# Attention of the first block inside the weight streams of its two projections

## The reference

```
x = x + 0.5*swiglu(rms_norm(x), ffn1)                   # g1, d1
proj = rms_norm(x) @ w_in          # 2048 -> 4608       # i1
qa (8 heads), ka (2), va (2), qd (4x2), kd (4x2) of 128; vd (4) of 256
qa, ka, qd, kd: rms_norm over 128 with a gain, then rotary (all 128, or the first 32)
out_a = softmax(qa ka^T / sqrt(128)) va                 # 8 heads
out_b = (softmax(qd0 kd0^T / sqrt(128)) - lam * softmax(qd1 kd1^T / sqrt(128))) vd
out_b = rms_norm(out_b) * subln * 0.8                   # 4 heads of 256
x = x + concat(out_a, out_b) @ w_out                    # o1
x = x + 0.5*swiglu(rms_norm(x), ffn2)                   # g2, d2
```

## Time and profile before

| | |
|---|---|
| median of 3 runs | 3600.59 us (3595.43 to 3614.2) |
| the profiled execution's own time | 3595.78 us |
| its span | 3594.0 us |
| PE, DVE, ACT, POOL busy | 94%, 64%, 42%, 1% of the span |
| mean granted TensorE clock | 0.972 of 2.4 GHz |
| time before the span and after it | 1.78 us |

### The profile page before, as it was taken

One profiled execution on the slowest core, in us unless ns is written; L12 is line 12 of the kernel. 1 busy time (PEld: TensorE's weight loads), 2 busy tenths in 40 slices (PEclk: granted clock), 3 DMA queues, 4 the chain that ended last, 5 costly groups with the idle time before them and its releaser, 6 DMA issues.

```text
span 3594.0 us, 40384 instructions
## 1 busy us (share of the span) xinstructions
PE 3384.7 (94%) x15130; PEld 2720.3 (76%) x15130; DVE 2306.3 (64%) x4078; ACT 1526.1 (42%) x2780; POOL 37.2 (1%) x37
## 2 busy tenths in 40 slices
PE   8999999999748999999999999999899988999898
PEld 6888878878637788887887788888567776888566
DVE  6788887765665688887777435555354346645565
ACT  5444444544334544444555322222254334422354
POOL 0000000000000000000000000000100000000100
PEclk9999999999978999999999999999899999999899
DMA  7777777766404677777786323333202235533314
GB/s 270 254 260 259 257 258 254 256 210 194 146 0 129 228 253 259 262 260 258 261 266 204 123 87 94 94 100 100 74 1 94 83 129 146 167 101 108 109 60 163
DMA packets 286920, 613.76 MB, mean 171 GB/s; under 512 B 19394, under 2 KB 23682, under 8 KB 284804
## 3 DMA queue, kind: packets, MB, share of 16 engines
q1 hardware_dynamic: 280804, 596.26, 51.2%
q0 software_dynamic: 1584, 8.39, 0.7%
q10 hardware_dynamic: 4336, 6.52, 0.5%
HBM read 604.80 MB, written 6.29 MB: 170 GB/s over the span
## 4 chain that ended last, share of the span: by engine, by line
PE 78%; DVE 10%; DMA 6%; ACT 3%; issue 2%; ACTq 0%; SPq 0%; DVEq 0%
PE acc L353 23%; PE acc L355 23%; PE acc L354 23%; DMA raw<-ffn_w_gu 5%; DVE lo L348 3%; PE acc L2017 2%; PE acc L2043 2%; ACT hi L344 1%; DVE cgw L1084 1%; PE tp L2030 1%; DVE mw L1086 1%; PE tp L1985 1%; PE tp L1681 0%; DMA raw<-ffn_w_down 0%; DVE tm L1576 0%
## 5 line engine op out<-in xcount | busy, mean ns | idle before, releaser
L348 DVE TENSOR_TENSOR lo<-raw,hi 128x512 fp32r<-128x512 f32 x1808 | 1208.5, 688 | 967.1 <-ACT hi L344 960.4
L344 ACT ACTIVATE hi<-raw 128x512 fp32r<-128x512 f32 x1808 | 1117.0, 630 | 1613.2 <-PE acc L355 1310.4
L353 PE MATMUL acc<-hi,hT_hi 128*128 128x512 f32 x1760 | 704.7, 400 | 30.4 <-DVE hT_lo L1071 14.6
L353 PE MATMUL acc<-hi,h_hi 128*128 128x512 f32 x1696 | 668.7, 394 | 23.3 <-DVE lo L348 18.2
L354 PE MATMUL acc<-hi,hT_lo 128*128 128x512 f32 x1760 | 689.4, 392 | 0.0
L355 PE MATMUL acc<-lo,hT_hi 128*128 128x512 f32 x1760 | 689.0, 391 | 0.0
L354 PE MATMUL acc<-hi,h_lo 128*128 128x512 f32 x1696 | 662.7, 391 | 0.0
L355 PE MATMUL acc<-lo,h_hi 128*128 128x512 f32 x1696 | 662.6, 391 | 0.0
L353 PEld LDWEIGHTS acc<-hi,hT_hi 128*128 128x128 f32 x1760 | 332.7, 189 | 121.9 <-DVE hT_lo L1071 22.1
L353 PEld LDWEIGHTS acc<-hi,h_hi 128*128 128x128 f32 x1696 | 319.7, 189 | 102.7 <-DVE lo L348 31.5
L355 PEld LDWEIGHTS acc<-lo,hT_hi 128*128 128x128 f32 x1760 | 332.8, 189 | 70.7
(11 more groups left out here) (244 smaller groups left out, 2282.8 us busy)
## 6 DMA issues: line engine op xcount, KB each, us to landing
raw<-ffn_w_gu SPq DMA_DIRECT2D x352, 512.0 KB, 5.5
raw<-w_in SPq DMA_DIRECT2D x280, 512.0 KB, 3.8
mw<-wmt SPq DMA_DIRECT2D x192, 512.0 KB, 5.2
raw<-ffn_w_down SPq DMA_DIRECT2D x176, 512.0 KB, 5.3
raw<-w_out SPq DMA_DIRECT2D x96, 512.0 KB, 4.2
ball<-rpbx SPq DMA_DIRECT2D x8, 768.0 KB, 8.6
x_rest<-x POOLq DMA_DIRECT2D x2, 2048.0 KB, 9.6
x<-x_rest SPq DMA_DIRECT2D x2, 2048.0 KB, 8.7
```

What stands on the lines that cost most here:

```text
L344: act.activation(hi[:, g % RING, :], raw_piece(g), ACT.Copy).then_inc(S["hi_made"], 1)
L348: dve.tensor_tensor(lo[:, g % RING, :], raw_piece(g), hi[:, g % RING, :].bitcast(F32), ALU.subtract).then_inc(S["lo_made"], 1)
L353: pe.matmul(bank, act_hi, hi[:, slot, :], start=start, stop=False)
```

## The change

The attention has no stage of its own. Its steps are called from `at1_side(s)` on PE, ACT and DVE, s counting 16 per chunk of i1 and going on into o1 (s = 144 + i in o1's piece i). Tables say at which piece each step stands. The chunks of i1 come in another order, o1 walks its pieces in another order, the norm's factor of a query is no longer multiplied into the query but given to the exponential as a scale per row, squares of heads go to ACT, gains are folded into the rotary tables once, scores and probabilities use the banks `cg` and `tp` in place of `acc`, the DMAs of `at1_consts` are issued by POOL.

```diff
+ORDER = (2, 0, 1, 5, 3, 6, 4, 7, 8)          # chunks of i1
+S_AT = (50, 56, 62, 68, 76, 84, 90, 96, 105, 109, 117, 121, 130, 133, 136, 139)   # scores(q)
+D_AT = (116, 128, 140, 146)                 # difference(h)
+V_AT = (131, 136, 146, 151)                 # diff_values(h)
+T_AT = (42, 43, 46, 63, 69, 80, 83, 97, 103, 112, 115, 124, 127)                  # heads_turn(g)
+O_PARTS = ((1, 0, 8), (0, 0, 8), (1, 8, 4), (0, 8, 4), (0, 12, 4), (1, 12, 4), (2, 0, 16), (3, 0, 16))
 # ACT
-                if j == 12:
-                    at1_consts()
 def exps(q): ...
-  ACT.Exp, bias=nm[:, q % 2, t:t + 1], scale=SCALE, ...
+  ACT.Exp, bias=nm[:, q % 2, t:t + 1], scale=qsd[:, t, col:col + 1], ...
+def head_square(pos, t, h): ...    # one 128x128 Square with its row sum, 52 in all
+def at1_side(s):                   # ACT
+    pos, r = s // 16 - 1, s % 16
+    if 0 <= pos <= 6 and (5 <= r <= 8 if pos else 5 <= r <= 6):  ... two head_square
+    if s == 23: ... activation(lam, Exp)
+    for e in now((44, 76, 108, 124), s): ... activation(qsd, Sqrt)
+    for g in now(T_AT, s - 5): ... activation(qkT, Copy)
+    for q in now(S_AT, s - 6): exps(q)
+    for q in now(S_AT[0:8], s - 11): pt_copy(q)
+    for q in now(S_AT[0:8], s - 15): head_hi(q)
+    for h in now(D_AT, s - 6): pt_copy(8 + h)
+    for k in now((147, 159), s): ... activation(obs, Sqrt)
+    for h in now((155, 156, 166, 167), s): ... activation(oT_hi, Copy)
 # DVE
+def axial_tables(k): ...  def partial_tables(k): ...     # s = 20 to 23
+def swapped(pos, t): ...           # 2 products, 256 elements a row each (64 for qd, kd)
+def rotated(pos, t): ...           # product of 512, sum of 512 (128 for qd, kd)
+def k_scaled(pos, t): ...          # keys alone are multiplied by their factor
+def at1_side(s):                   # DVE
+    if s == 19: dve.wait_ge(S["rope_in"], 16 * 13) ... lambda sums
+    if pos == 0 and r in (8, 9): ... swapped(0, r - 8); rotated(0, r - 8)
+    if 1 <= pos <= 6 and 7 <= r <= 10: ... swapped or rotated, in turn
+    for q in now(S_AT, s - 5): maxes(q)
+    for q in now(S_AT[0:8], s - 7): normalise(q)
+    for q in now(S_AT[0:8], s - 16): head_out(q)
+    for h in now(D_AT, s): difference(h, 0)
+    for h in now(D_AT, s - 1): difference(h, 1)
+    for h in now(V_AT, s - 5): diff_out(h)
+    for h in now(V_AT, s - 6): diff_squares(h)
+    ...
 # PE
+def at1_side(s):
+    for g in now(T_AT, s): heads_turn(g)
+    for q in now(S_AT, s): scores(q)
+    for q in now(S_AT[0:8], s - 6): turn_p(q, pr1[0][:, q % 2])
+    for q in now(S_AT[0:8], s - 10): head_values(q)
+    for h in now(D_AT, s - 1): turn_p(8 + h, pr1[h % 2][:, 0])
+    for h in now(V_AT, s): diff_values(h)
+    for h in now((150, 151, 161, 162), s): diff_turn(h)
-pe.wait_ge(S["roped"], 1)          # and all of at1 between the streams
+for c, kt0, n in O_PARTS:          # o1
+    if kt0 == 0 and c == 1:
+        pe.wait_ge(S["oh_lo"], A_HEADS)
+    elif kt0 in (8, 12):
+        pe.wait_ge(S["tg_lo"], g0 + (2 if kt0 == 8 else 4))
+    ...
+    for cx in now((33, 40, 52), i): x_turn(phases["n3"], cx, ...)
 # POOL, behind gain_load(0) and ahead of ctx_load(0)
+pool.wait_ge(S["mod_done"], MODS)
+pool.dma_start(ropa[:, 0], ...)    # the 13 DMAs of at1_consts
```

More of the change, by code:

```diff
@@ L223, in build @@
         lam = keep("lam", [P, 8])
+        sm1 = keep("sm1", [P, 4, 2])
         mx = keep("mx", [P, 2, 2])
@@ L501, in _ @@
             load_down(down[0], phases["d1"], 6 * FC)
-            load_wide(win1, phases["i1"], 0, 9)
-            load_wide(wout1, phases["o1"], 0, 4)
+            for k, c in enumerate(ORDER):
+                load_wide(win1, phases["i1"], c, 1, False, k)
+            o_unit = phases["o1"].pieces // 2
+            for c, kt0, n in O_PARTS:
+                for u in range(n // 2):
+                    unit(o_unit, wout1[c, kt0 // 2 + u])
+                    o_unit += 1
             load_gu(gu[1], phases["g2"], MODS)
@@ L692, in _, with exps @@
             stream(phases["d1"].pieces, 4, DK, after=d1_side)
+            g0 = phases["at1"].groups
+            def exps(q):
+                act.wait_ge(S["m_ready"], q + 1)
+                if 2 <= q < 10:
+                    act.wait_ge(S["cg_done"], q - 1)
+                elif q >= 12:
+                    act.wait_ge(S["cg_done"], 9 + (q - 12) // 2)
+                rows, sums = p_rows(q)
+                for t in range(2):
+                    col = q_col(q)
+                    ins = act.activation(rows[:, t], cg[q % 2][:, t * L:(t + 1) * L], ACT.Exp,
+                                         bias=nm[:, q % 2, t:t + 1], scale=qsd[:, t, col:col + 1],
+                                         accum_out=sums[:, t:t + 1])
+                ins.then_inc(S["p_made"], 1)
@@ L767, in _ @@
-            stream(phases["o1"].pieces, 4, after=o1_side)
+            stream(phases["i1"].pieces, 9, after=lambda c, j: (i1_side(c, j), at1_side(16 * c + j)))
+            for i in range(LOOK, 64 + LOOK):
+                hi_piece(act, phases["o1"].pieces + i)
+                at1_side(9 * 16 + i)
+                if i == 35:
+                    act.wait_ge(S["hq_made"], 52)
+                for c in now((35, 40, 53), i):
+                    act.wait_ge(S["acc_taken"], phases["o1"].taken + 2 * (c + 1))
+                    x_squares(c)
+                for c in now((38, 45, 57), i):
+                    x_hi(phases["n3"], 2, c)
@@ L1180, in i1_side @@
                     dve.wait_ge(S["rs_made"], norms[0])
[L1182 to L1192, removed]
-                    link(ins)
@@ L1194, in _ @@
[L1194 to L1204, removed]
@@ new lines, in both_tiles, with axial_tables @@
+            def both_tiles(v, n):
+                return v.unsqueeze(1).broadcast_to([P, 2, n])
+            def axial_tables(k):
+                g = gbc[:, k].rearrange("p (b s n) -> p b s n", b=2, s=2)
+                dve.tensor_tensor(tA[:, k, 0], ropa[:, 0], both_tiles(gbc[:, k], HD), ALU.mult)
+                for t in range(2):
+                    dst, sn = (v.rearrange("p (b s n) -> p b s n", b=2, s=2) for v in (tA[:, k, 1, t], ropa[:, 1, t]))
+                    for hf in range(2):
+                        ins = dve.tensor_tensor(dst[:, :, hf, :], sn[:, :, hf, :], g[:, :, 1 - hf, :], ALU.mult)
+                link(ins)
@@ new lines, in partial_tables @@
+            def partial_tables(k):
+                g = gbc[:, 2 + k]
+                dve.tensor_tensor(tBc[:, k, :, 0:32], ropb[:, 0], both_tiles(g[:, 0:32], 32), ALU.mult)
+                dve.tensor_copy(tBc[:, k, :, 32:HD], both_tiles(g[:, 32:HD], HD - 32))
+                for hf in range(2):
+                    d0, d1 = 16 * hf, 16 * (1 - hf)
+                    ins = dve.tensor_tensor(tBs[:, k, :, d0:d0 + 16], ropb[:, 1, :, d0:d0 + 16],
+                                            both_tiles(g[:, d1:d1 + 16], 16), ALU.mult)
+                link(ins)
@@ new lines, in rotated @@
+            def rotated(pos, t):
+                nh, k, x = 4 if pos else 2, int(pos in (0, 3, 5)), qk_src(pos, t)
+                xv = x.rearrange("p (h n) -> p h n", n=HD)
+                cs = tA[:, k, 0, t] if pos < 3 else tBc[:, k, t]
+                link(dve.tensor_tensor(xv, xv, cs.unsqueeze(1).broadcast_to([P, nh, HD]), ALU.mult))
+                w = HD if pos < 3 else 32
+                ins = dve.tensor_tensor(xv[:, :, 0:w], xv[:, :, 0:w], rp2[:, 0:nh * w].rearrange("p (h n) -> p h n", n=w),
+                                        ALU.add)
+                if t == 1 and pos not in (0, 3, 5):
+                    ins.then_inc(S["roped"], 1)
+                else:
+                    link(ins)
@@ L1311, in x_add @@
+            stream(phases["i1"], 9, 2, proj_take, after=lambda c, j: (i1_side(c, j), at1_side(16 * c + j)))
             def x_add(c, t):
@@ L1313, in x_add @@
                 dve.tensor_tensor(xv, acc[2 * (c % 2) + t][:], xv, ALU.add).then_inc(S["acc_taken"], 1)
-            def o1_side(c, j):
-                if c and j == 8:
-                    x_lo(phases["n3"], 2, c - 1)
-            stream(phases["o1"], 4, 2, x_add, after=o1_side)
+            for i in range(LOOK, 64 + LOOK):
+                lo_piece(dve, phases["o1"].pieces + i)
+                at1_side(9 * 16 + i)
+                for c in now((39, 46, 58), i):
+                    x_lo(phases["n3"], 2, c)
+                for c in now((29, 33, 49, 65), i):
+                    for t in range(2):
+                        o_done_at(dve, phases["o1"], c, t)
+                        x_add(c, t)
             def second_lap(j):
@@ L1819, in turn_p @@
                 ins.then_inc(S["cg_done"], 1)
-            g0 = phases["at1"].groups
             def head_values(q):
-                pe.wait_ge(S["cg_taken"], 14 + q)
-                if q >= 2:
-                    pe.wait_ge(S["oh_lo"], q - 1)
-                c0 = VA_COL + q // 4 * HD
+                pe.wait_ge(S["cg_taken"], q + 1)
+                wait(pe, "oh_lo", q)
```

(43 more changed lines are left out.)

422 lines of the change are left out of this document (268 added, 154 removed).

## The result

The median fell from 3600.49 us (3595.43 to 3614.2, 4 runs) to 3500.07 us (3494.59 to 3507.94, 4 runs): ratio 0.9717, 95% interval 0.9684 to 0.975. The profiled execution is the longest of the four, 3507.94 us with a span of 3506.0.

A forecast was written before the change was run, and what follows sets the result against it. PE bounds the streams, a chain of round trips the attention. −136.0 − 3.0 − 5.3 + 43 + 4 = −97.3 us, from the profiled 3595.78 to 3498.5, so a median of 3500; range 3488 to 3524.

The forecast's parts named there:

- The hole: PE's gap between i1's last matmul and o1's first, over the attention: removed in full, −136.0 us.
- the slow start of o1: o1's first 20 pieces, whose first matmuls run at the lower clock level: removed, −3.0 us.
- ACT's issues: 13 DMA issues on ACT in i1's chunk 0, stopping PE, then half rate: moved to POOL, −5.3 us.
- PE's side work: Attention transposes, scores and values on PE within the streams, not hidden: +43 us, between 39.7 and 45.4.
- Stops: PE stops in the new stream where DVE or ACT bursts run late: +4 us, bounds 0 and 28.
- The stop of `turn_p(0)`: PE after piece 56, where turning the first probabilities waits for the normalisation: about 1.2 us.
- The stop after pieces 20 to 25: DVE's tables and chunk 0's rotary run some 3.2 us late, so PE stops for about 0.6 us.
- DVE by totals: Busiest chunk of i1, pieces 66 to 81: DVE 22.8 us beside PE's 27.9, 82%, as in g1.
- the cushion: How late DVE's `lo` may be before PE stops, with a ring of four pieces: 2.6 us.
- POOL: 13 constant DMAs on POOL land by 775 us, DVE asks about 787: hidden, 12 us to spare; late constants 2%.
- The lower clock level: Rival, pieces 42 to 168: stops keep PE at 1.2 GHz, time 3694, slower by 98 us; chance 4%.
- The rivals: DVE and ACT can't keep up (20%), constants late (2%), attention's end late for o1 (2%), lower clock stays (4%).

The follow-up runs named there:

- e5: Kernel before, with only the 13 small DMAs issued by POOL: stage 426.21 us against 432.41, median 3598.18 us.
- e1: Changed kernel with the 13 small DMAs issued by ACT again, after piece 12 of i1's first chunk: stage 337.45 us against 331.78, median 3506.41 us.
- e2: Changed kernel with each of the 16 score products made twice on PE: stage 344.48 us against 331.78, median 3534.21 us.
- e3: Changed kernel with each of the 16 row maxima made four times on DVE: stage 346.63 us against 331.78, median 3522.02 us.
- e11: Changed kernel with each of the 16 row maxima made twice on DVE: stage 333.54 us against 331.78, median 3507.10 us.
- e12: Changed kernel with each of the 16 row maxima made six times on DVE: stage 372.81 us against 331.78, median 3546.17 us.
- e4: Changed kernel, probabilities of the 8 plain heads transposed 4 pieces behind the scores instead of 6: stage 357.04 us against 331.78, median 3526.55 us.
- e6: Changed kernel with an unused square root on ACT ahead of each of 16 exponentials, forcing table loads: stage 347.06 us against 331.78, median 3515.65 us.
- e9: Changed kernel run again, unedited: stage 331.78 us, the same, median 3506.91 us.
- e7: Changed kernel with one unused DVE product of 512 elements a row more for each of 8 query tiles: stage 331.82 us against 331.78, median 3508.76 us.
- e8: Changed kernel with conditioning rows loaded early by POOL and their Silu moved on ACT: stage 331.84 us against 331.78, median 3497.35 us.
- e10: The kernel of e8 again, in more rounds, against the changed kernel: stage 331.85 us against 331.78, median 3498.46 us.

## Why the prediction was right

The forecast was 3500 for a median of 3500.07. So close a hit is luck. Medians of the same kernel came out 7 us apart. And −97.3 from the median of 3600.59 is 3503.3; the forecast took a lower starting point, the profiled execution's 3595.78, and part of the way back, and that choice happened to make up for the stops counted too high. The stage is the fair test: −97.3 forecast, −100.6 measured.

- *The hole, 136.0, and the slow start of o1, 3.0*: gone in full; there is no distance over 0.24 us at the seam, and the clock is 1.00.
- *ACT's issues, 5.3*: shown by e5, 5.5 in i1 with the stop and the half-rate matmuls as counted. e1's 5.7 confirms the size only: no half-rate spell, and late weights instead.
- *PE's side work, 43*: what is left of 331.8 after 208 pieces at 1.360 (282.9), four x turns (3.6), the stops (2.2) and about 0.3 more behind the first stop is 42.8. e2 shows that such work adds in full. The choice of 43 between 39.7 and 45.4 was right.
- *Stops, 4*: the term that was mis-sized. With its first 1.2 us counted among what i1 has anyway, it measured 1.0. The stop of `turn_p(0)` was worked out as 1.2 and is there with 1.03. The stop after pieces 20 to 25 (0.6) didn't come, nor did the small ones. There the tables took 1.0, 1.0, 0.6 and 0.6 us where 1.3, 1.3, 0.8 and 0.8 were counted, and the `lo` of piece 26 still ended 0.39 ahead of its first matmul (801.78, 802.17), from 2.46 before the burst. These stops, 3.0 us, and the issues explain the 3.3 us.
- *DVE by totals*: pieces 66 to 81 were taken for the busiest, with 22.8 us in 27.9, 82%. They have 20.7 in 28.2, 74%. The busiest chunk is another, pieces 16 to 31, with 18.5 us in 21.8, 85%, since PE has no side work there to make it longer, and it passes without a stop. In e1, where the ring enters it late, the small delays fall there. With e3, e11 and e12 that confirms that the burst against the cushion is the right question.
- *POOL*: the first constant was issued at 760.5 and the wait of DVE did not show. The 13 issues took 0.54 to 0.72 us each, as the few at other times, and DVE's seven `lo` beside them a median of 0.686 (0.687 in g1). The contention over a shared SBUF interface that the Trainium skill names (GPSIMD Engine Reference, Key points) isn't seen here.
- *The lower clock level* didn't stay. e4 and e12 show how it would begin: with waits of several microseconds among the pieces, the clock of the stage goes to 0.98 and 0.97, and what the stage grew by beyond the added waits is 8.2 us beside 17.0 of them (e4) and 16.0 beside 25.0 (e12, about 10 of it by the clock), not the doubling of all pieces. The length of one stop doesn't tell: behind 2.43 us in e6 (at 849.17) seven matmuls in a row stood at twice the distance, behind 2.93 us in e1 none did.

I had said that ACT would load ten tables, and that PE would have no gap over 2 us between i1 and o1 and wait for `pr` in single microseconds: all three hold. The rivals fell by rows: waits 2.2 us, clock 1.00, constants in time, and no wait for `oT_lo` in o1.

Outside the stage the profiled execution of the change is 13 us slower than that of the kernel before: 2.4 ahead of i1, 6.0 in g2 and d2, 4.3 behind. Nothing of the change runs there but the POOL queue's order. g2 and d2 take 756 to 764 us over the twelve profiles that leave them alone, and behind d2 e9, the same kernel, is within 1 us of the kernel before, so I take it for the spread of runs. It is why the whole time of that execution fell by 88 us only.

## What to carry to other kernels

A stage of short round trips between two streams that are bound by one engine is worth its whole length less that engine's own work in it, if the other engines' additions fit as bursts between the pieces: compare each burst with ring depth times piece time less the latency of making a piece, not the busy share with 100%, and add up bursts that stand within a few pieces (e3's, 2.2 us each, are under the cushion of 2.5 and still stop PE where they meet others). Place a consumer so many pieces behind its producer that the round trip is over, and count what stands in front of the producer in the same slot (table loads, squares); two pieces less cost 25 us here. DMA issues belong on a queue whose engine makes nothing for the stream: 13 of them on ACT cost 5 to 6 us.

## What the runs showed that I had not expected

The stage is the same to 0.07 us in five profiles (331.78, 331.78, 331.82, 331.84, 331.85) of the change, e9, e7, e8 and e10, while the rest of the program moves by 10 us and more. In e2 both runs, 3532.49 and 3535.93, are some 20 us longer than the stage explains. In the one that has a profile, 19 of these lie behind d2 (1662.9 us against 1640.8 to 1648.4 in the other kernels shown here), in the second layer's last attention, whose instructions are the same. A stretch of 100 us there, in e2, then in the first profile of the change, then in e6, the same time after d2:

```profile
3271.10:3371.10 100.00, 81.86 (x262) 50.59 (x260) 42.44 (x118) 31.75 (x67) 14.69 (x9) 0.62 0.14 51
```

```profile
3257.60:3357.60 100.00, 83.34 (x333) 52.50 (x334) 46.94 (x141) 37.92 (x83) 14.70 (x9) 0.73 0.11 42
3269.40:3369.40 100.00, 82.33 (x375) 51.64 (x376) 51.06 (x157) 40.88 (x91) 14.65 (x9) 0.83 0.12 44
```

The granted clock is 0.62, 0.73 and 0.83, and PE gets through 262, 333 and 375 matmuls. The change run again (e9) has 0.83 and 360 there, so the same kernel shows two of these levels. What makes the clock fall further in one execution than in another stays open, and whether e2's edit has a part in it isn't shown; for a change of some 10 us it means that a stage that can be cut out of the profile says more than the whole time.
